# Rotary embedding in one mixer: tables that carry the norm's factors, and two tiles in work

## The chip, the cores and the metric

The kernel runs on one core of a Trainium2 chip. The metric is the device time of one execution in microseconds, as the median of several runs. The engines are TensorE (PE; its weight loads are PEld), VectorE (DVE), ScalarE (ACT), GpSimd (POOL) and the DMA queue of SyncE (SP). Each works through its instructions in program order; they meet at semaphores.

## The reference, cut to what matters

The whole computation is a transformer of several blocks on 16 + 512 tokens: two hybrid layers, then two more mixers, each followed by an MLP and an embedding gate. The change touches one mixer alone, the first of the second half. There the normed input is multiplied by a matrix of 3072 columns; queries and keys of two attentions (4 heads with two maps of 64, and 8 heads of 64) get a rotary embedding over their 64 dimensions:

```python
def rms(x, g):
    y = xf * lax.rsqrt(jnp.mean(xf * xf, axis=-1, keepdims=True) + EPS) * g

def rope_2(x, pos):                      # cos, sin: (position, 32)
    x1, x2 = x[..., :half], x[..., half:]
    return jnp.concatenate([x1 * cos - x2 * sin, x1 * sin + x2 * cos], axis=-1)
```

The first attention takes the difference of two softmax maps per head (a paired attention), the second is a dilated one.

## The kernel before

Activations lie transposed in SBUF: 128 features by up to 528 tokens. A product is computed in fp32 accuracy from two halves: weights and activations are split into a high part and a low part, and each step of a product is three matmuls (high x high, low x high, high x low), lines 1807 to 1809, for outputs of features by tokens, or 1803 to 1805 for outputs of tokens by features (the values). One *step* takes one block of 128 input features; a tile of 128 output features by 512 tokens has eight steps, that is 24 matmuls, in one PSUM bank.

Weights come in panels of 128x512. ScalarE makes the high part of a panel (L1247), VectorE the low part (L1426), TensorE uses it. `begin_panel(j)` puts the split of panel j + 2 into both queues, so a split stands in these queues behind whatever was put there first. A product of one 128-column tile has two panels; a value product (`gemm_tok`, four tiles of tokens by 512 columns, 96 matmuls) has eight.

One function, `schedule`, walks the whole program, and each engine keeps its own part of what `do(...)` names, in that order. `mark()` notes how much each engine has been given up to there; waiting on an engine's mark means waiting until it has done all of that.

The norm's factors (one for each token, the row tile `rs`) are not applied to the input: they are multiplied into each product as it leaves PSUM. For queries and keys this is part of `rope64` (L450). For a tile it issues:

- on ScalarE (L1310): a copy of the tile from PSUM to the second half of `tmp` (L1315), and four copies of 32 partitions each, with neighbouring groups of 32 exchanged, to the first half (L1317). They wait for the product, and for VectorE's mark `prior`, which is all that VectorE was given before. The bank is free when the copies are done.
- on VectorE (L1470): straight part times cos (L1474), crossed part times sin (L1475), their sum (L1477), and the sum times `rs` into the query or key tile (L1479).

All tiles use the same two halves of `tmp`. The mixer (`mixer_ab`, L953) has 16 such tiles. Four query tiles (Q) are computed together by `chunk_major`, under the norm's sums; `lead` (L283) then puts out their four rotary parts and lets four steps of the key products (K) run after each of them. The order of the rotary tiles is Q0 K0 Q1 Q2 K1 Q3 K2 K3. Two value products follow. Then `attend` (L322) runs the paired attention in 16 units of one head and 128 queries, and between their scores, transposes and products it lets steps of `others()` (L1018) run: the eight rotary tiles of the second attention, 64 steps in all. There the VectorE part of a tile is held back in the list `later` until four steps of the next product are out. During this attention the steps use two PSUM banks in turn, elsewhere seven.

In the attention VectorE takes scores with mask and minimum from PSUM (L1626), ScalarE makes exponentials (L1355), VectorE mixes the two maps (L1677 to L1681), TensorE transposes (L1869), VectorE and ScalarE in turn copy the transposes to `PT` (L1640, L1366), and TensorE multiplies with the values (L1881).

The same `rope64` serves the two hybrid layers, which the change leaves as they are.

Of the kernel before, what the change touches and what calls it, by code (L numbers as in the profile page):

```python
# [8 lines left out]
ALU = mybir.AluOpType  # L9
AF = mybir.ActivationFunctionType  # L10
# [4 lines left out]
S = 512  # L15
# [73 lines left out]
def schedule(m, PP, does):  # L89
# [351 lines left out]
    rs = m["rs"]  # L441
# [8 lines left out]
    def rope64(ps, dst, a, b, t, before, later=None):  # L450
# [7 lines left out]
        else:  # L458
            later.append(rest)
        return ("act", "rope64 in", n)  # L460

    def rope32(ps, row, dst, a, b, t, r, before):
# [490 lines left out]
    def mixer_ab(hr, N, produce):  # L953
# [4 lines left out]
        def rotated(dst, o, c, later=None):  # L958
            def evac(ps, a, b, t):
                return rope64(ps, dst[:, o + c, :], a, b, t, before, later=later)  # L960
            return evac
# [256 lines left out]
def scalar_program(act, panels, m, A):  # L1218
# [91 lines left out]
    def rope64_in(it):  # L1310
# [5 lines left out]
        for x in range(4):  # L1316
            e.activation(it.p[32 * x:32 * x + 32], it.ps[32 * (x ^ 1):32 * (x ^ 1) + 32, :], AF.Copy).then_inc(*act.up("rope64 in", it.n))  # L1317

    def zgate(it):
        act.wait_ge("dve", "evac", it.n)  # L1320
        e.activation(it.g, it.zz, AF.Tanh, scale=0.5).then_inc(*act.up("zgate", it.n))
# [73 lines left out]
    def mark(it):  # L1395
        act.note("mark", it.n)

    does = {"mark": mark, "load": load, "load p": load_p, "load lam": load_lam, "split": split, "square": square, "sqrt soon": sqrt_soon, "norm_col": norm_col, "norm_rows": norm_rows,
            "high": high, "copy_out": copy_out, "four_out": four_out, "two_heads": two_heads, "rope64 in": rope64_in, "zgate": zgate, "gate": gate,
            "forget exp": forget_exp, "forget ln": forget_ln, "relu2": relu2, "ple": ple, "scores": scores, "turn": turn, "turn_v": turn_v,  # L1400
# [8 lines left out]
def vector_program(dve, panels, m):  # L1409
# [60 lines left out]
    def rope64(it):  # L1470
# [7 lines left out]
        dve.wait_ge("dve")  # L1478
        e.tensor_tensor(it.dst, it.p, it.rs, ALU.mult).then_inc(*dve.up("rope64", it.n))  # L1479

    def rope32(it):
# [261 lines left out]
    def mark(it):  # L1743
        dve.note("mark", it.n)

    does = {"mark": mark, "load": load, "split": split, "norm_col": norm_col, "norm_rows": norm_rows, "add squares": add_squares, "low": low, "normed": normed, "scale_out": scale_out,
            "two_heads": two_heads, "rope64": rope64, "rope32": rope32, "straight": straight, "crossed": crossed, "zgate": zgate, "gate": gate,
            "proj": proj, "add_quarter": add_quarter, "forget in": forget_in, "forget sum": forget_sum, "forget rows": forget_rows,
# [314 lines left out]
```

## Time and profile before

| | us |
|---|---|
| median of 3 runs | 3099.63 |
| lowest, highest | 3090.12, 3103.06 |
| the profiled execution | 3102.26 |
| its span, first to last instruction | 3100.1 |

| engine | busy us | share of the span | instructions |
|---|---|---|---|
| TensorE, matmuls | 2851.4 | 92% | 15420 |
| TensorE, weight loads | 2380.8 | 77% | 15420 |
| VectorE | 1598.8 | 52% | 3374 |
| ScalarE | 1227.8 | 40% | 2672 |
| GpSimd | 32.2 | 1% | 32 |

A matmul's row reaches beyond the start of the next, since matmuls are pipelined; the distance of two starts tells what one costs. "Idle before" is the time in which an engine stood still before an instruction, with the instruction that released it. The granted clock (PEclk) is the share of full speed that TensorE was given; its mean over the whole execution is 0.949. The chain of waits is followed back from the last instruction, at each step to what released it, so that its shares tell which engine set the end. The mixer's rotary tiles lie between 1516 and 1728 us of the span.

### The profile page before, as it was taken

Reading aid. Unit: us, or ns where it says so; the run is one execution under the profiler, and the core shown is the slowest. Engines: PE = TensorE matmul, PEld = TensorE weight load, DVE = VectorE, ACT = ScalarE, POOL = GpSimd, SP = SyncE. Lnnn points to the kernel's source line nnn. Section 1 sums busy time; section 2 is a strip of 40 time slices with the busy share of each in tenths; the row PEclk is TensorE's granted clock in tenths of the full one; section 3 lists DMA queues with packets and bytes.
Section 4 is the critical chain, followed back from the end, with each engine's and each line's share of the span. In section 5 each row is a group of like instructions: output and inputs, shape, how many; then the busy total and the mean of one; then the engine's idle time right before and its main releaser. Section 6 shows DMA issues by size and latency. Waiting matters only on the chain.

```text
span 3100.1 us, 40010 instructions
## 1 busy us (share of the span) xinstructions
PE 2851.4 (92%) x15420; PEld 2380.8 (77%) x15420; DVE 1598.8 (52%) x3374; ACT 1227.8 (40%) x2672; POOL 32.2 (1%) x32
## 2 busy tenths in 40 slices
PE   7998998999999998999698889999997789899998
PEld 7888988899888777778575567888775477778886
DVE  6354555555444554555447554444556754534445
ACT  3335334433233534433446543333343344433333
POOL 0000000000000000000000000000000000000000
PEclk9999999999998999999898899999997589999999
DMA  3201112122210212223121122333221011233332
GB/s 125 73 21 59 55 42 72 52 76 88 80 52 21 76 44 65 65 75 96 51 77 34 31 65 85 96 95 95 82 70 47 3 40 35 68 94 97 97 96 87
DMA packets 116989, 207.83 MB, mean 67 GB/s; under 512 B 14016, under 2 KB 25152, under 8 KB 116672
## 3 DMA queue, kind: packets, MB, share of 16 engines
q1 hardware_dynamic: 115648, 201.09, 21.6%
q10 hardware_dynamic: 1152, 4.20, 0.4%
q8 instruction: 121, 1.98, 0.3%
q14 instruction: 68, 0.56, 0.1%
HBM read 203.07 MB, written 2.10 MB: 66 GB/s over the span
## 4 chain that ended last, share of the span: by engine, by line
PE 73%; DVE 15%; ACT 9%; issue 2%; DMA 0%; SPq 0%; DVEq 0%; ACTq 0%
PE pp L1807 18%; PE pp L1809 18%; PE pp L1808 17%; PE pp L1881 5%; PE pp L1857 4%; DVE wl L1426 3%; PE pp L1869 2%; ACT tmp L1317 2%; ACT wh L1247 2%; PE pp L1803 1%; PE pp L1804 1%; PE pp L1805 1%; ACT P L1355 1%; PE pp L1914 1%; DVE st L1732 1%
## 5 line engine op out<-in xcount | busy, mean ns | idle before, releaser
L1807 PE MATMUL pp<-Hh,wh 128*128 128x512 f32 (+1 forms) x2322 | 885.1, 381 | 115.7 <-DVE wl L1426 68.8
L1808 PE MATMUL pp<-Hl,wh 128*128 128x512 f32 (+1 forms) x2322 | 813.8, 350 | 0.0
L1809 PE MATMUL pp<-Hh,wl 128*128 128x512 f32 (+1 forms) x2322 | 813.6, 350 | 0.0
L1426 DVE TENSOR_TENSOR wl<-raw,wh 128x512 fp32r<-128x512 f32 (+2 forms) x786 | 507.2, 669 | 459.5 <-ACT wh L1247 446.9
L1807 PEld LDWEIGHTS pp<-Hh,wh 128*128 128x128 f32 x2322 | 454.5, 196 | 220.8 <-DVE wl L1426 81.9
L1247 ACT ACTIVATE wh<-raw 128x512 fp32r<-128x512 f32 (+2 forms) x786 | 454.6, 603 | 264.3 <-PE pp L1809 203.8
L1808 PEld LDWEIGHTS pp<-Hl,wh 128*128 128x128 f32 x2322 | 455.0, 196 | 57.6 <-issue 9.0
L1809 PEld LDWEIGHTS pp<-Hh,wl 128*128 128x128 f32 x2322 | 452.9, 195 | 54.4
L1807 PE MATMUL pp<-Yh,wh 128*128 128x512 f32 (+1 forms) x1280 | 481.5, 376 | 6.7 <-DVE Yl L1446 5.7
L1808 PE MATMUL pp<-Yl,wh 128*128 128x512 f32 (+1 forms) x1280 | 459.0, 359 | 0.0
L1809 PE MATMUL pp<-Yh,wl 128*128 128x512 f32 (+1 forms) x1280 | 458.9, 359 | 0.0
L1355 ACT ACTIVATE P<-P,st 128x256 f32<-128x256 f32 (+7 forms) x280 | 149.9, 535 | 401.9 <-DVE st L1626 401.6
L1807 PEld LDWEIGHTS pp<-Yh,wh 128*128 128x128 f32 x1280 | 242.2, 189 | 51.3 <-DVE Yl L1446 8.0
L1809 PEld LDWEIGHTS pp<-Yh,wl 128*128 128x128 f32 x1280 | 241.8, 189 | 35.7
L1808 PEld LDWEIGHTS pp<-Yl,wh 128*128 128x128 f32 x1280 | 242.4, 189 | 34.1 <-issue 2.2
L1881 PEld LDWEIGHTS pp<-V,PT 128*128 128x128 f32 x1600 | 224.4, 202 | 25.4 <-DVE O L1654 7.2
L1881 PE MATMUL pp<-V,PT 128*128 128x64 f32 (+1 forms) x1600 | 225.3, 277 | 6.1 <-DVE O L1654 3.7
L1857 PE MATMUL pp<-K,Q 64*128 64x256 f32 (+16 forms) x624 | 200.2, 478 | 21.6 <-DVE Z L1523 8.5
L1869 PE MATMUL pp<-con,P 128*128 128x128 f32 x616 | 121.6, 288 | 28.6 <-DVE PT L1640 17.7
L1869 PEld LDWEIGHTS pp<-con,P 128*128 128x128 f32 x616 | 79.1, 146 | 65.6 <-DVE PT L1640 25.0
L1340 ACT ACTIVATE Yh<-tmp 128x512 fp32r<-128x512 f32 x64 | 40.4, 632 | 189.7 <-DVE tmp L1583 189.7
L1857 PEld LDWEIGHTS pp<-K,Q 64*128 64x128 f32 (+2 forms) x624 | 82.6, 203 | 36.6 <-issue 24.9
(219 smaller groups left out, 2672.4 us busy)
## 6 DMA issues: line engine op xcount, KB each, us to landing
raw<-in_w SPq DMA_DIRECT2D x700, 256.0 KB, 2.7
raw<-in_w SPq DMA_DIRECT2D x46, 192.0 KB, 2.4
raw<-in_w SPq DMA_DIRECT2D x40, 128.0 KB, 2.0
out<-X SPq DMA_DIRECT2D x8, 256.0 KB, 2.0
con<-in_con ACTq DMA_DIRECT2D x1, 1576.0 KB, 11.5
X<-in_x SPq DMA_DIRECT2D x2, 528.0 KB, 5.8
X<-in_x ACTq DMA_DIRECT2D x2, 528.0 KB, 6.9
Z<-in_p ACTq DMA_DIRECT2D x2, 512.0 KB, 3.3
```

Of the source, the lines that this page charges most:

```text
L1247: e.activation(part("wh", j), landing(j), AF.Copy).then_inc(*act.up("split", j))
L1317: e.activation(it.p[32 * x:32 * x + 32], it.ps[32 * (x ^ 1):32 * (x ^ 1) + 32, :], AF.Copy).then_inc(*act.up("rope64 in", it.n))
L1340: e.activation(it.hi, it.q, AF.Square).then_inc(*act.up())
L1355: e.activation(p.p, p.p, AF.Exp, bias=p.neg, scale=-1.0, accum_out=p.sum).then_inc(*act.up("exp", it.u))
L1426: e.tensor_tensor(part("wl", j), landing(j), part("wh", j).bitcast(F), ALU.subtract).then_inc(*dve.up("split", j))
L1732: e.max(it.best, it.score).then_inc(*dve.up())
L1807: e.matmul(it.ps, wh, xh, start=it.first, stop=False)
L1808: e.matmul(it.ps, wh, xl, start=False, stop=False)
L1809: e.matmul(it.ps, wl, xh, start=False, stop=it.end).then_inc(*pe.up())
L1857: e.matmul(p.sc, p.q, p.k[:, p.cut:it.ext], start=True, stop=True).then_inc(*pe.up("scores", it.u, x))
L1869: e.transpose(it.b4[:, 128 * x:128 * x + 128], it.p[:, o:o + 128], it.ident).then_inc(*pe.up("turn", it.u))
L1881: done = e.matmul(it.o, p, v, start=x == 0, stop=x == n - 1)
```

## The change

A second form of the rotary step is used in this mixer only. Before the mixer's first tile, VectorE multiplies the cos and the sin table (512 tokens each) by `rs` in place: two operations of 128x512. A tile then needs four copies on ScalarE (the crossed ones, `halves in`), and three operations on VectorE (`rope halves`): crossed part times sin in place, the product's bank times cos into the query or key tile, and the sum of both. The straight copy and the multiplication by `rs` are gone.

The tiles use the two halves of `tmp` in turn. ScalarE's copies of a tile wait for the product and for the sum of the tile two before; those of the first two tiles wait for the tables. VectorE's first operation waits for the copies and for its own last operation. The bank is free when the operation that reads it (`rope straight`) is done.

```diff
+    def rope_scaled(ps, dst, a, b, t, before, later=None):
+
+        x = ropes["n"] % 2
+        p = tmp[:, x, 0:b - a]
+        n = do("halves in", ps=ps, p=p, t=t, prior=ropes["begin"] if ropes["n"] < 2 else None, given=ropes.get(x))["n"]
+        ropes["n"] += 1
+        ropes[x] = n
+
+        def rest():
+            do("rope halves", ps=ps, p=p, cos=cos[:, a:b], sin=sin[:, a:b], dst=dst, n_in=n, before=before)
+        if later is None:
+            rest()
+        else:
+            later.append(rest)
+        return ("dve", "rope straight", n)
...
         def rotated(dst, o, c, later=None):
             def evac(ps, a, b, t):
-                return rope64(ps, dst[:, o + c, :], a, b, t, before, later=later)
+                if "begin" not in ropes:
+                    do("ropes", tables=[cos[:, 0:S], sin[:, 0:S]], rs=rsS)
+                    ropes["begin"] = mark()
+                return rope_scaled(ps, dst[:, o + c, :], a, b, t, before, later=later)
...
+    def halves_in(it):
+        act.wait_ge(*it.t)
+        if it.prior is not None:
+            for other in ("dve", "pe"):
+                act.wait_ge(other, "mark", it.prior)
+        if it.given is not None:
+            act.wait_ge("dve", "rope halves", it.given)
+        for x in range(4):
+            e.activation(it.p[32 * x:32 * x + 32], it.ps[32 * (x ^ 1):32 * (x ^ 1) + 32, :], AF.Copy).then_inc(*act.up("halves in", it.n))
...
+    def ropes(it):
+        for table in it.tables:
+            e.tensor_tensor(table, table, it.rs, ALU.mult).then_inc(*dve.up())
+
+    def rope_halves(it):
+        dve.wait_ge("act", "halves in", it.n_in)
+        for other in ("pe", "act", "pool"):
+            dve.wait_ge(other, "mark", it.before)
+        dve.wait_ge("dve")
+        e.tensor_tensor(it.p, it.p, it.sin, ALU.mult).then_inc(*dve.up())
+        e.tensor_tensor(it.dst, it.ps, it.cos, ALU.mult).then_inc(*dve.up("rope straight", it.n_in))
+        dve.wait_ge("dve")
+        e.tensor_tensor(it.dst, it.dst, it.p, ALU.add).then_inc(*dve.up("rope halves", it.n_in))
```

## Rows read from the trace of the kernel before

**Rows 1.** the page, part 4: the chain that ended last, shares by engine

```profile
PE 73%; DVE 15%; ACT 9%; issue 2%; DMA 0%; SPq 0%; DVEq 0%; ACTq 0%
```

**Rows 2.** busy time by stretch (start:end, length, engines' busy us, PEclk, DMA share)

```profile
1516.40:1561.20 44.80, 22.61 (x73) 16.62 (x72) 21.83 (x34) 24.83 (x42) 0.00 (x0) 0.77 0.08 23
1561.20:1606.70 45.50, 45.48 (x192) 37.00 (x192) 14.36 (x26) 18.75 (x30) 0.00 (x0) 0.96 0.36 105
1606.70:1728.50 121.80, 92.72 (x392) 63.72 (x392) 81.63 (x192) 71.93 (x150) 0.00 (x0) 0.87 0.13 35
```

**Rows 3.** chain of work from 1516.4 to 1561.2, its shares by line

```profile
by line: ACT tmp L1317 36.9%; DVE tmp L1477 11.0%; DVE tmp L1474 10.8%; issue 9.7%; DVE tmp L1475 9.6%; ACT tmp L1315 9.1%; DVE wl L1426 7.8%; DVE Q L1479 3.3%; PE pp L1803 1.5%; ACT rs L1273 1.3%; PE pp L1836 0.3%; DVE K L1479 0.2%; DVEq L
```

**Rows 4.** groups, 1516.4 to 1561.2: line, count, busy, mean, idle before

```profile
L1807 PE MATMUL pp<-Hh,wh 128*128 128x512 f32 x24 | 12.3, 513 | 20.2 <-DVE wl L1426 20.2
...
L1315 ACT ACTIVATE tmp<-pp 128x512 f32<-128x512 f32 x7 | 4.2, 597 | 16.8 <-DVE wl L1426 11.1 <-DVE Q L1479 5.8
```

**Rows 5.** timeline, ScalarE: start, length (us), what, [idle before, releaser]

```profile
1516.44 0.60 ACT L1273 ACTIVATE rs<-pp 128x512 f32<-128x512 f32 x1 [2.14 <-PE pp L1836]
1516.93 0.59 ACT L1315 ACTIVATE tmp<-pp 128x512 f32<-128x512 f32 x1
...
1522.86 0.60 ACT L1315 ACTIVATE tmp<-pp 128x512 f32<-128x512 f32 x1 [2.88 <-DVE Q L1479]
1523.48 2.42 ACT L1317 ACTIVATE tmp<-pp 32x512 f32<-32x512 f32 x4
1525.93 0.63 ACT L1247 ACTIVATE wh<-raw 128x512 fp32r<-128x512 f32 x1
```

**Rows 6.** timeline, VectorE, first query tile and the split after the second tile

```profile
1520.08 0.69 DVE L1474 TENSOR_TENSOR tmp<-tmp,con 128x512 f32<-128x512 f32 x1 [5.57 <-ACT tmp L1317]
1520.69 0.69 DVE L1475 TENSOR_TENSOR tmp<-tmp,con 128x512 f32<-128x512 f32 x1
1521.41 0.69 DVE L1477 TENSOR_TENSOR tmp<-tmp 128x512 f32<-128x512 f32 x1
1522.13 0.69 DVE L1479 TENSOR_TENSOR Q<-tmp,rs 128x512 f32<-128x512 f32 x1
...
1528.60 0.68 DVE L1426 TENSOR_TENSOR wl<-raw,wh 128x512 fp32r<-128x512 f32 x1
```

**Rows 7.** timeline, TensorE, matmuls at either level and the first value product

```profile
1530.36 0.63 PE L1809 MATMUL pp<-Hh,wl 128*128 128x512 f32 x1
1530.79 0.63 PE L1807 MATMUL pp<-Hh,wh 128*128 128x512 f32 x1
...
1536.14 0.40 PE L1808 MATMUL pp<-Hl,wh 128*128 128x512 f32 x1
1536.37 0.40 PE L1809 MATMUL pp<-Hh,wl 128*128 128x512 f32 x1
...
1561.17 0.69 PE L1803 MATMUL pp<-wh,Hh 128*128 128x512 f32 x1 [2.00 <-DVE wl L1426]
```

**Rows 8.** one line's instructions: count, duration ns min/median/max, starts, form

```profile
L1460 DVE TENSOR_TENSOR Q<-pp,rs x5: 681/684/693, 2299.0 to 2303.9; 128x512 f32<-128x512 f32 x5
```

**Rows 9.** groups of the attention stretch, 1606.7 to 1728.5

```profile
L1426 DVE TENSOR_TENSOR wl<-raw,wh 128x512 fp32r<-128x512 f32 x16 | 11.0, 690 | 29.6 <-ACT wh L1247 29.5
...
L1315 ACT ACTIVATE tmp<-pp 128x512 f32<-128x512 f32 x8 | 4.8, 596 | 4.3 <-DVE PT L1640 1.5 <-DVE M L1681 1.4 <-PE pp L1809 1.1
```

**Rows 10.** timeline, ScalarE, before the second tile's copies in the attention

```profile
1627.98 0.19 ACT L1355 ACTIVATION_READ_ACCUMULATOR M<-M,st 128x1 f32 x1
1628.59 0.60 ACT L1315 ACTIVATE tmp<-pp 128x512 f32<-128x512 f32 x1 [0.42 <-DVE M L1681]
```

**Rows 11.** timeline, TensorE, first step of the product after tile 2

```profile
1625.55 0.39 PE L1807 MATMUL pp<-Hh,wh 128*128 128x512 f32 x1
```

**Rows 12.** timeline, VectorE, second operation of tile 1 in the attention

```profile
1621.53 0.69 DVE L1475 TENSOR_TENSOR tmp<-tmp,con 128x512 f32<-128x512 f32 x1
```

**Rows 13.** chain of work, 1606.7 to 1728.5, the piece at the seventh tile

```profile
1716.84 1.12 PE pp L1889 x4
```

More of the change, by code:

```diff
@@ L460, in rope64 @@
         return ("act", "rope64 in", n)
+    ropes = {"n": 0}
+    def rope_scaled(ps, dst, a, b, t, before, later=None):
[11 more added lines that the diff above has]
+        return ("dve", "rope straight", n)
     def rope32(ps, row, dst, a, b, t, r, before):
@@ L1398, in scalar_program @@
     does = {"mark": mark, "load": load, "load p": load_p, "load lam": load_lam, "split": split, "square": square, "sqrt soon": sqrt_soon, "norm_col": norm_col, "norm_rows": norm_rows,
-            "high": high, "copy_out": copy_out, "four_out": four_out, "two_heads": two_heads, "rope64 in": rope64_in, "zgate": zgate, "gate": gate,
+            "high": high, "copy_out": copy_out, "four_out": four_out, "two_heads": two_heads, "rope64 in": rope64_in, "halves in": halves_in, "zgate": zgate, "gate": gate,
             "forget exp": forget_exp, "forget ln": forget_ln, "relu2": relu2, "ple": ple, "scores": scores, "turn": turn, "turn_v": turn_v,
@@ L1746, in vector_program @@
     does = {"mark": mark, "load": load, "split": split, "norm_col": norm_col, "norm_rows": norm_rows, "add squares": add_squares, "low": low, "normed": normed, "scale_out": scale_out,
-            "two_heads": two_heads, "rope64": rope64, "rope32": rope32, "straight": straight, "crossed": crossed, "zgate": zgate, "gate": gate,
+            "two_heads": two_heads, "rope64": rope64, "ropes": ropes, "rope halves": rope_halves, "rope32": rope32, "straight": straight, "crossed": crossed, "zgate": zgate, "gate": gate,
             "proj": proj, "add_quarter": add_quarter, "forget in": forget_in, "forget sum": forget_sum, "forget rows": forget_rows,
```

## The prediction

> **What bounds the kernel now.** The page comes first: TensorE holds 73% of the chain that ended last, VectorE (DVE) and ScalarE (ACT) 24% together [rows 1]. So a gain can only lie where those two carry the chain. The change touches the first mixer of the second block alone, so I looked at that by stretches [rows 2]: from 1516.4 to 1561.2 us TensorE is busy for 22.6 of 44.8 us; from 1561.2 to 1606.7, where the two value products run, it is never idle; from 1606.7 to 1728.5, the paired attention with eight more rotary tiles beside it, it is busy for 92.7 of 121.8 us. The middle stretch has nothing to give.
>
> In the first stretch the chain is nearly all rotary work: the four crossed copies (L1317) 36.9%, the straight copy (L1315) 9.1%, the VectorE lines 1474 to 1479 most of the rest, TensorE under 2% [rows 3]. TensorE waits 20.2 us there for split weights (L1426), and the straight copies wait 16.8 us for VectorE [rows 4]. The reader is to see a ring with one tile in it: ACT copies five times (0.62 + 2.45 us), VectorE works through four operations, and only then does ACT start the next tile; the weight splits stand in the same two queues behind the tiles, so TensorE gets a panel only once per turn. Start to start a tile takes 1522.86 - 1516.93 = 5.9 us, with a split about 6.5 [rows 5, 6].
>
> **First stretch, step by step.** Durations: four crossed copies 2.45 us, one split on ACT 0.65 [rows 5], on VectorE 0.69; a VectorE operation with no wait in front starts 0.61 after the one before, with a wait 0.72 [rows 6]. The new tile is sin (no predecessor in the way), cos 0.61 later, the sum 0.72 later, 0.69 long: 2.02 us against 2.74 from 1520.08 to the end of L1479. New here is that cos reads PSUM. The nearest row is an operation of the same shape that takes PSUM and a table, 684 ns [rows 8], as long as the one from SBUF [rows 6], so I take no difference; the ends are 681 and 693 ns. The Trainium skill, page "VectorE: DVE Perf Modes", section on the TRN2 errata, speaks against this edit: it gives a PSUM source 120 fixed cycles against 58 for SBUF, an estimate of 0.065 us an operation, some 0.9 us over all tiles on the path. The trace does not show that difference.
>
> The tables: two operations of 128x512, placed before the first tile, whose copies wait for them. The norm's row copy ends at 1517.04 [rows 5], so they run to about 1517.1 + 0.61 + 0.69 = 1518.4, and the first copy starts at 1518.45 instead of 1516.93. Nothing hides these 1.5 us; queued behind the waiting ACT is all that follows. The scaled tables serve no later reader with other needs.
>
> From there both queues can be written down, since ACT no longer waits for the tile before (a tile waits for the sum of the tile two before, in its own half of tmp). The order is Q0 K0 split Q1 split Q2 K1 split Q3 split K2 split. ACT: seven tiles of 2.45 and five splits of 0.65 from 1518.45, so K2's copies end at 1538.2. VectorE needs 2.0 a tile and follows about 2 us behind: Q0 is done at 1522.95 and Q1 starts on ACT at 1524.0, Q1 is done at 1528.5 and K1 starts at 1529.55, and so on; no slot holds ACT up, the nearest margin being about 1 us. The splits reach TensorE at 1526.1, 1529.2, 1534.8, 1537.9 and 1541.0; the last is the one that the value product waits for, at 1561.17 before [rows 7]. TensorE itself has two panels of twelve matmuls after 1534.8. A matmul starts every 0.23 us at the granted 2.4 GHz and every 0.43 at 1.2 GHz [rows 7]. All at the higher level it is done in time (1540.7), all at the lower one at 1545.0. TensorE still pauses 2 to 4 us between panels, so I take the mean grant of this stretch before, 0.77 [rows 2]: 24 x 0.23 / 0.77 = 7.2 us, and the value product at 1542.0. The gain is 19, with bounds of 16 and 20.2. Late next is then TensorE.
>
> ACT's last key tile falls beside the value product as before, 5.3 us from copies to the next split against 6.4; two value panels take 5.5, so that stays covered. PSUM banks come free with cos on VectorE instead of with the copies on ACT: with seven banks in turn the first reuse is the last key tile, long after.
>
> **Attention stretch.** Its chain is ACT and VectorE in alternation, one rotary tile for every second head: the copies keep the weight split behind them in ACT's queue, VectorE stands at that split's low half 29.6 us in total [rows 9], and the scores queue behind it. On this chain each of eight tiles loses the straight copy, 8 x 0.62 = 5.0 us. Each loses one of four VectorE operations: the intervals 0.61 + 0.72 + 0.72 + 0.61 become 0.11 (a new wait in front) + 0.61 + 0.72 + 0.61, so 0.61 less; seven of the eight lie on the chain, while at the seventh tile it runs through the transposes instead [rows 13]: 4.3 us. Third, the copies no longer wait for all that VectorE has queued, softmax mixing and PT copies included: 4.3 us of idle time before L1315, of which 1.1 was TensorE's and stays [rows 9]; one such wait is the 0.42 us at 1628.59, where ACT had ended its exponentials and the product had ended before [rows 10, 11]. Of the 3.1 I take 2.5, since at the first tile the product ends just as the copies start. Sum: 5.0 + 4.3 + 2.5 = 11.8.
>
> A new wait comes in: in this stretch the steps have two banks, so the product after next waits for cos, which is held back for four steps, while before it waited for the copies. The product after tile 1 starts at 1625.55 [rows 11], and the second VectorE operation of tile 1 ends at 1621.53 + 0.69 = 1622.2 [rows 12]. This is 3.3 us of cover, and cos itself comes earlier now. I cost it at nothing; if TensorE ran two steps further ahead it would show. Bounds for the stretch: 5 (cover gone, or TensorE late) and 13.2.
>
> **Sum.** 19 + 11.8 = 31 us, 1.0%. The profiled execution took 3102.3 us with a span of 3100.1; it would become about 3071. The median of before is 3099.6, so 3069 is the forecast, and its runs lie between 3090 and 3103.
>
> **Rivals.** *The slots free nothing.* If ACT still had to wait for the tile before in both stretches (through order in the queues, or banks), only the removed operations count: seven tiles x 1.23 - 1.5 = 7.1, and 9.3 in the attention: 16.4, time 3083. For it speaks that each queue is strictly in order; against it, that the walk above finds every wait met. Chance 0.07.
>
> *TensorE takes over in the attention.* It is idle 29.1 us of that stretch and the change asks for 11.8 of them, but the granted clock there is 0.87 [rows 2]. Were it 0.80, its work would be 8 us longer, which leaves 4 of the gain: 19 + 4, time 3077. Against it: VectorE hardly waits for a product in this stretch. Chance 0.13.
>
> *Slower, by the clock.* The grant falls after TensorE idled, and each matmul started at the lower level costs 0.20 us more [rows 7]. The value products have 192 matmuls, nearly all at the higher level [rows 2], and the attention's steps 192 more. If the new, denser pattern of short pauses left the lower level standing through them, 155 matmuls undo the gain, and from 235 the kernel is slower by over 0.5%; all 384 give +77 - 31, time 3146. Against it: the change takes away idle time of TensorE, and before, after waits of 20.2 us in all, the level was low at 1530.36 and high again at 1536.14 [rows 4, 7]. Chance 0.03.
>
> The forecast has the remaining 0.77.
>
> **How the numbers follow.** Best ends together: 20.2 + 13.2 + 1.8 (the value products at a grant of 1.00 instead of 0.96, 45.5 x 0.04 [rows 2]) = 35, time 3064; worst: 16 + 5 = 21, time 3079. With the scatter of the runs shown that gives 3057 to 3084, which takes in the first two rivals. A measurement of this kernel can tell about 0.5%, here 15.5 us, so faster means under 3084: 0.88; within 0.5%: 0.09, mostly the first rival's upper side; slower 0.03.
>
> **What would show it.** In the profile after: (1) copies of the first two query and key tiles back to back, starting about 1.5 us after the norm's rows; (2) the value product at about 25 us after that row copy instead of 44; (3) the product with cos at 0.68 to 0.69 us; (4) in the attention VectorE's idle time before the split's low half down from 29.6 to near 22, and no TensorE wait for the line of cos; (5) a stretch of about 110 us. The forecast is wrong if TensorE waits there for VectorE's cos, if copies still start only after the sum of the tile before, or if the granted clock falls in the value products.

## The result, and the profile after

The changed kernel takes **3073.15 us** (median of five runs, 3066.20 to 3079.09) against 3099.63 for the one before (five runs of the same comparison): ratio 0.9914, 95% interval 0.9895 to 0.9933, which is 26.5 us less. The profiled execution took 3075.13 us with a span of 3073.3. Two later comparisons of the same kernel gave 0.9884 and 0.9875; what lies between these figures has a section below.

The page of after, part 4 (shares of the chain that ended last):

```profile
PE 75%; DVE 14%; ACT 8%; issue 2%; DMA 0%; SPq 0%; DVEq 0%; ACTq 0%
```

VectorE and ScalarE together go from 24% [rows 1] to 22% of a span that is 27 us shorter, so what went away came out of their part of the chain. The same three stretches as [rows 2], in after (start:end, length, then busy us and count for PE, PEld, DVE, ACT, POOL, then granted clock, DMA share, GB/s):

```profile
1516.10:1540.56 24.46, 18.90 (x73) 14.08 (x72) 18.27 (x29) 20.80 (x36) 0.00 (x0) 0.93 0.15 43
1540.56:1584.40 43.84, 43.82 (x192) 35.96 (x192) 13.78 (x25) 18.12 (x29) 0.00 (x0) 1.00 0.37 108
1584.40:1693.60 109.20, 84.34 (x392) 58.75 (x392) 76.74 (x184) 67.11 (x142) 0.00 (x0) 0.97 0.14 39
```

The same work took 44.8, 45.5 and 121.8 us before. In the first of them ScalarE goes from 42 to 36 instructions and VectorE from 34 to 29, and ScalarE is now busy for 20.8 of 24.5 us. The granted clock rose in all three: 0.77 to 0.93, 0.96 to 1.00, 0.87 to 0.97.

From here on I read every kernel by three distances that don't depend on where the window is cut: **first** is from the end of the norm's row copy [rows 5] to the first value product [rows 7], **values** from there to the first score matmul of the paired attention, **attention** from there to the first score of the second attention. Before they are 44.13, 46.34 and 121.03, sum 211.5. After they are 23.83, 44.64 and 108.43, sum 176.9.

ScalarE's timeline of after over the first stretch (start, length in us, engine and line, what, [idle before, releaser]; L1348 are the crossed copies, L1268 the high half of a split):

```profile
1516.13 0.60 ACT L1294 ACTIVATE rs<-pp 128x512 f32<-128x512 f32 x1 [2.14 <-PE pp L1881]
1518.10 4.88 ACT L1348 ACTIVATE tmp<-pp 32x512 f32<-32x512 f32 x8 [1.36 <-DVE con L1514]
1523.00 0.63 ACT L1268 ACTIVATE wh<-raw 128x512 fp32r<-128x512 f32 x1
1523.65 2.42 ACT L1348 ACTIVATE tmp<-pp 32x512 f32<-32x512 f32 x4
1526.10 0.63 ACT L1268 ACTIVATE wh<-raw 128x512 fp32r<-128x512 f32 x1
1526.76 4.88 ACT L1348 ACTIVATE tmp<-pp 32x512 f32<-32x512 f32 x8
```

After the 1.36 us for the two scaled tables there is no idle bracket left: Q0's and K0's copies stand together as one row of eight. Compare [rows 5], where 2.88 us lie between two tiles. VectorE in the same stretch (L1521 sin, L1522 cos from PSUM, L1524 sum, L1457 low half of a split):

```profile
1520.56 0.69 DVE L1521 TENSOR_TENSOR tmp<-tmp,con 128x512 f32<-128x512 f32 x1 [2.50 <-ACT tmp L1348]
1521.16 0.68 DVE L1522 TENSOR_TENSOR Q<-pp,con 128x512 f32<-128x512 f32 x1
1521.88 0.69 DVE L1524 TENSOR_TENSOR Q<-Q,tmp 128x512 f32<-128x512 f32 x1
1523.00 0.69 DVE L1521 TENSOR_TENSOR tmp<-tmp,con 128x512 f32<-128x512 f32 x1 [0.43 <-ACT tmp L1348]
...
1524.94 0.68 DVE L1457 TENSOR_TENSOR wl<-raw,wh 128x512 fp32r<-128x512 f32 x1
...
1539.82 1.29 DVE L1457 TENSOR_TENSOR wl<-raw,wh 128x512 fp32r<-128x512 f32 x2
```

From the second tile on VectorE waits 0.4 to 0.5 us for each tile's copies, so ScalarE alone now sets the pace: 2.42 a tile and 0.63 a split, with hardly a gap. On TensorE, the pause ahead of the fourth of the five panels and the step to the value product (same columns):

```profile
1534.34 0.50 PE L1852 MATMUL pp<-Hh,wh 128*128 128x512 f32 x1 [1.29 <-DVE wl L1457]
1534.68 0.39 PE L1853 MATMUL pp<-Hl,wh 128*128 128x512 f32 x1
1534.91 0.40 PE L1854 MATMUL pp<-Hh,wl 128*128 128x512 f32 x1
...
1540.09 0.39 PE L1854 MATMUL pp<-Hh,wl 128*128 128x512 f32 x1
```

The starts are 0.23 us apart after the first, the upper level of [rows 7], and the granted clock from 1534.34 to 1540.56 us is 1.00. The end of the chain of waits over this stretch (start, length, who) tells what released the value product:

```profile
1539.56 0.25 PE pp L1854
1539.82 0.69 DVE wl L1457
1540.52 0.04 issue
1540.56 0.50 PE pp L1848
```

TensorE was through with its last key panel at about 1540.3, and the split for the value product ended at 1540.5: the split is the last to arrive, by 0.2 us. TensorE's waits for split weights, 1516.1 to 1540.6 (us in total, times, longest), against the 20.2 of [rows 4]:

```profile
PE pp L1852 <- DVE wl L1457: 5.4, 2, 4.1
```

Groups of the attention stretch of after, 1584.4 to 1693.6 (count | busy us, mean ns | idle before, releasers), beside [rows 9]:

```profile
L1348 ACT ACTIVATE tmp<-pp 32x512 f32<-32x512 f32 x32 | 18.8, 588 | 2.0 <-PE pp L1854 1.3
L1457 DVE TENSOR_TENSOR wl<-raw,wh 128x512 fp32r<-128x512 f32 x16 | 11.0, 690 | 22.8 <-ACT wh L1268 22.7
L1522 DVE TENSOR_TENSOR Q<-pp,con 128x512 f32<-128x512 f32 x4 | 2.7, 685 | 0.0
```

The idle time ahead of ScalarE's copies fell from 5.1 us (4.3 ahead of the straight ones, 0.8 ahead of the crossed ones) to 2.0; of what is left 1.3 us is a wait for TensorE, the rest gaps of 0.02 us, and no wait for VectorE is named; the wait at the split's low half fell from 29.6 to 22.8.

### The profile page after: what moved, and what is told of

It reads as the page before. It is cut to its first block, busy times and chain, and to the rows that moved or that the text cites. A ratio compares the mean times of both kernels' runs of the same rounds, so it can differ in the third digit from the quotient of the medians.

```text
span 3073.3 us, 39979 instructions
## 1 busy us (share of the span) xinstructions
PE 2850.2 (93%) x15420; PEld 2381.4 (77%) x15420; DVE 1589.5 (52%) x3360; ACT 1218.5 (40%) x2656; POOL 32.0 (1%) x32
## 3 DMA queue, kind: packets, MB, share of 16 engines
q8 instruction: 121, 1.98, 0.3%
## 4 chain that ended last, share of the span: by engine, by line
PE 75%; DVE 14%; ACT 8%; issue 2%; DMA 0%; SPq 0%; DVEq 0%; ACTq 0%
PE pp L1852 19%; PE pp L1854 18%; PE pp L1853 18%; PE pp L1926 5%; PE pp L1902 4%; DVE wl L1457 2%; PE pp L1914 2%; ACT wh L1268 1%; PE pp L1848 1%; PE pp L1850 1%; PE pp L1849 1%; PE pp L1959 1%; ACT tmp L1348 1%; ACT P L1386 1%; DVE st L1777 1%
## 5 line engine op out<-in xcount | busy, mean ns | idle before, releaser
L1457 DVE TENSOR_TENSOR wl<-raw,wh 128x512 fp32r<-128x512 f32 (+2 forms) x786 | 507.1, 668 | 456.8 <-ACT wh L1268 442.5
L1268 ACT ACTIVATE wh<-raw 128x512 fp32r<-128x512 f32 (+2 forms) x786 | 454.7, 603 | 264.1 <-PE pp L1854 206.2
L1637 DVE TENSOR_TENSOR M<-pp,M 128x512 f32<-128x512 f32 x56 | 38.7, 692 | 139.0 <-PE pp L1854 138.0
```

Source lines behind the costliest of these rows:

```text
L1268: e.activation(part("wh", j), landing(j), AF.Copy).then_inc(*act.up("split", j))
L1457: e.tensor_tensor(part("wl", j), landing(j), part("wh", j).bitcast(F), ALU.subtract).then_inc(*dve.up("split", j))
L1637: e.tensor_tensor(it.y, it.ps, it.y, ALU.add).then_inc(*dve.up("evac", it.n))
```

## The experiments

The theory: the first stretch gains about 19 us, from a ring with one tile in it that becomes two full queues; the attention gains about 12, from one copy and one VectorE operation less for each tile, and from a wait for VectorE's whole queue that became a wait for one instruction. The rivals that the runs had to exclude: only the removed operations count; the overlap alone counts; the later stretches take or give something of their own.

| kernel | median us (n) | ratio to before, 95% | first | values | attention | of it the last wait | sum |
|---|---|---|---|---|---|---|---|
| before | 3099.63 (5) | | 44.13 | 46.34 | 121.03 | 1.15 | 211.5 |
| after | 3073.15 (5) | 0.9914, 0.9895 to 0.9933 | 23.83 | 44.64 | 108.43 | 0.90 | 176.9 |
| after_again | 3062.63 (4) | 0.9884, 0.9850 to 0.9917 | 23.84 | 44.68 | 107.55 | 0.02 | 176.1 |
| after_paired | 3067.46 (6) | 0.9875, 0.9848 to 0.9903 | 23.85 | 44.66 | 108.62 | 1.09 | 177.1 |
| lead_only | 3079.04 (6) | 0.9936, 0.9907 to 0.9964 | 23.85 | 44.64 | 121.06 | 0.90 | 189.6 |
| attention_only | 3086.04 (10) | 0.9969, 0.9946 to 0.9991 | 44.15 | 46.33 | 110.03 | 1.07 | 200.5 |
| one_tile | 3081.03 (10) | 0.9934, 0.9913 to 0.9956 | 33.70 | 44.64 | 108.61 | 1.07 | 187.0 |
| queue_wait | 3077.80 (8) | 0.9926, 0.9901 to 0.9952 | 23.85 | 44.65 | 111.73 | 1.36 | 180.2 |
| straight_copy | 3078.74 (8) | 0.9930, 0.9900 to 0.9959 | 28.21 | 44.68 | 113.65 | 1.98 | 186.5 |
| plain_tables | 3067.23 (3) | 0.9915, 0.9855 to 0.9975 | 25.46 | 44.70 | 113.71 | 0.35 | 183.9 |
| early_tables | 3065.14 (3) | 0.9913, 0.9866 to 0.9960 | 22.51 | 44.64 | 109.34 | 1.80 | 176.5 |
| all_rotary | 3049.34 (5) | 0.9815, 0.9790 to 0.9839 | 22.52 | 44.64 | 109.21 | 1.66 | 176.4 |

The first two rows are one comparison. Three later ones had their own runs of before, with medians of 3103.40 (21 runs), 3098.20 (17) and 3105.27 us (10). The first of them holds after_again, one_tile, attention_only and lead_only, the second queue_wait, straight_copy, plain_tables and early_tables, the third after_paired and all_rotary. The whole times scatter by 6 to 25 us within a kernel. Much of that comes before the mixer: its row copy ends anywhere from 1503.2 to 1519.6 us in the eleven profiles in which everything ahead of it is the same. The distances repeat within 0.02 us in the first stretch, 0.07 in the values and about 1.1 in the attention.

The attention's scatter has one place. The *last wait* in the table is the idle time of ScalarE ahead of its copies for the eighth and last rotary tile, whose product TensorE is still computing. These copies and that idle time, in after_again, after and early_tables:

```profile
1686.12 2.42 ACT L1348 ACTIVATE tmp<-pp 32x512 f32<-32x512 f32 x4
1689.01 2.42 ACT L1348 ACTIVATE tmp<-pp 32x512 f32<-32x512 f32 x4 [0.90 <-PE pp L1854]
1676.91 2.42 ACT L1348 ACTIVATE tmp<-pp 32x512 f32<-32x512 f32 x4 [1.80 <-PE pp L1854]
```

The granted clock from the copies of the seventh tile to these is 1.00, 0.85 and 0.72:

```profile
1675.55:1686.12 10.57, 6.73 (x35) 5.10 (x33) 6.26 (x11) 6.31 (x11) 0.00 (x0) 1.00 0.08 31
1677.56:1689.01 11.45, 6.80 (x29) 5.16 (x27) 7.05 (x12) 6.31 (x11) 0.00 (x0) 0.85 0.11 30
1664.57:1676.91 12.34, 7.68 (x29) 5.83 (x27) 7.04 (x12) 6.31 (x11) 0.00 (x0) 0.72 0.07 26
```

Without this wait the attention takes 107.53 us in each of the three executions of after, and 107.54 to 107.55 in one_tile, early_tables and all_rotary; before takes 119.88. So the attention too can be compared to some hundredths of a microsecond, and I call this its *net* distance. The distances carry the verdicts below, and the ratios say only that the wholes agree with them.

**after_again and after_paired** are the changed kernel unedited, run beside the kernels of the first and of the third later comparison.

> The changed kernel once more, nothing edited, to tell what belongs to it from what belongs to one execution. The local gain of 34.6 us (first product stretch 20.3, value products 1.7, attention 12.6) should come back within 0.5 us in the first and third part, which no TensorE level decides. My theory of the missing 8 us (two later stretches of 435 and 438 us, the same instructions in both kernels, took 3.9 us more each at a lower granted clock) says that these differ from execution to execution: in this profile they should lie anywhere between 435 and 442 us, and the kernel at 3066 to 3079 us. The rival says that the change causes them, by moving what follows against the clock's rhythm: then they are 438.8 and 441.5 us again.

> The changed kernel beside the next one, with more rounds, for the size of its gain over many executions. Expected from the parts: 34.6 to 35.4 us off the mixer in every execution, while later stretches scatter by some us with the granted clock: median about 35 us under that of the kernel before, ratio 0.989. If the 26.5 us of the first comparison were the whole gain, the ratio would be 0.9915 again.

Measured: 176.1 and 177.1 against 176.9. The gain in the mixer is 34.4 to 35.4 us in all three executions, whatever the whole shows. Two expectations missed: after_again's attention is 0.9 us shorter than after's, where I had allowed 0.5 (it is the last wait, 0.02 against 0.90), and its whole times, 3060 to 3066 us, lie below the 3066 to 3079 that I had named. The interval of after_paired, 0.9848 to 0.9903, excludes the 0.9915 of its rival.

**lead_only and attention_only** each do one half of the change: the new form for the tiles of the first attention alone (o == 0), or of the second alone (o == 4). In lead_only the attention's tiles still go through `rope64`, on tables that carry the norm's factor already, so the factor enters twice in them; the operations and their order are those of before. In attention_only the tables are scaled at the first tile inside the attention, and the scaling has a wait for VectorE's own last operation in front (not in the excerpt).

```diff
         def rotated(dst, o, c, later=None):
             def evac(ps, a, b, t):
+                if o == 4:      # lead_only; attention_only has o == 0
+                    return rope64(ps, dst[:, o + c, :], a, b, t, before, later=later)
                 if "begin" not in ropes:
```

> The new form in the first stretch only; the attention's eight tiles take the old five copies and four operations (their output carries the norm's factor twice, since the tables are scaled). Theory: first stretch 23.8 us, attention 121.0 us, time about 3099.6 - 20.3 - 1 = 3078. Rival: attention shorter than 118 us although its work is the old one, which would put part of its gain down to the earlier start.

> The eight tiles of the first stretch keep the old five copies and four operations, the tables are scaled when the attention's first tile comes. Theory (the two gains are independent and add up): first stretch 44.1 us, attention 108.4 us plus up to 1.4 for the tables' two operations, time about 3099.6 - 11 = 3088. Rival (the attention gained only because it began in another state): attention near 121 us, time 3100.

Measured: lead_only 23.85 and 121.06, attention_only 44.15 and 110.03. Each has one half at the value of after and the other at that of before (lead_only's net attention, 120.16, within 0.3 us). attention_only pays for the tables there: its net attention is 108.96, 1.4 us over that of after; its values last 46.33 as before, so the 1.7 us that the value products gain belong to the first stretch. The granted clock goes with it; attention_only, first stretch and values:

```profile
1504.90:1549.45 44.55, 22.71 (x71) 16.60 (x71) 21.80 (x34) 24.64 (x42) 0.00 (x0) 0.73 0.09 24
1549.45:1595.78 46.33, 45.51 (x192) 37.05 (x193) 14.39 (x26) 19.45 (x31) 0.00 (x0) 0.96 0.35 103
```

With the old first stretch the value products start after TensorE idled half of the time, and their mean grant is 0.96; in after it is 1.00, from the first matmul.

**one_tile** keeps the new operations but gives every tile the same half of `tmp`, so a tile's copies wait for the sum of the tile before.

```diff
-        x = ropes["n"] % 2
+        x = 0
...
-        n = do("halves in", ps=ps, p=p, t=t, prior=ropes["begin"] if ropes["n"] < 2 else None, given=ropes.get(x))["n"]
+        n = do("halves in", ps=ps, p=p, t=t, prior=ropes["begin"] if ropes["n"] < 1 else None, given=ropes.get(x))["n"]
```

> All tiles use the same half of tmp, so ScalarE's copies of a tile wait for the sum of the tile before; tables and operation counts stay. Theory (overlap is most of the gain in the first stretch, and nothing of it in the attention, where one tile comes every 13 to 16 us): from the norm's rows to the value product 37 us (44.1 less 7 x 1.23, plus 1.5 for the tables) instead of 23.8, attention 108.4 as before, time 3086. Rival (removed operations are the gain, in either stretch): first stretch stays at about 24 to 26 us, time 3073 to 3076.

Measured: 33.70 in the first stretch, 108.61 in the attention. So the second half of `tmp` is worth 9.9 us where tiles stand in a row and nothing in the attention (net 107.54 against 107.53). The first figure is 3.3 us under what I expected. ScalarE and VectorE of one_tile show why, from the second tile on:

```profile
1511.35 2.43 ACT L1348 ACTIVATE tmp<-pp 32x512 f32<-32x512 f32 x4 [2.09 <-DVE Q L1524]
1513.80 0.63 ACT L1268 ACTIVATE wh<-raw 128x512 fp32r<-128x512 f32 x1
1515.86 2.42 ACT L1348 ACTIVATE tmp<-pp 32x512 f32<-32x512 f32 x4 [1.43 <-DVE K L1524]
```

```profile
1515.13 0.69 DVE L1524 TENSOR_TENSOR K<-K,tmp 128x512 f32<-128x512 f32 x1
1515.74 0.68 DVE L1457 TENSOR_TENSOR wl<-raw,wh 128x512 fp32r<-128x512 f32 x1
```

A turn takes 1515.86 - 1511.35 = 4.5 us, copies to copies. The copies start when the sum ends (1515.13 + 0.69), while the split's low half (1515.74) is still running. Before, the copies waited for VectorE's mark, and the split stood under it: of the 16.8 us that they waited, 11.1 were for L1426 [rows 4]. I had taken only the removed operations out of the ring and left the low half in it. The seven turns, from copies to copies and the last to the value product, took 5.93, 6.46, 6.46, 5.93, 6.46, 6.52 and 6.48 us before and take 4.52, 4.51, 4.51, 4.58, 4.51, 4.57 and 5.14 here. The two turns without a split lose 1.35 to 1.41 us, which is the copy's 0.62 and the 0.72 of the fourth operation; my 1.23 had counted 0.61 for that one. The last turn loses 1.34, although it holds a split, because the value product itself waits for its low half. The other four lose 1.95 each, so the narrower wait takes out 0.6 in each of them. Of the 3.3 us some 1.0 is thus the removed work, which I had priced too low, and 2.3 the narrower wait. No run puts the old wait back in this stretch, so this split between the two rests on the turns alone. Both together are worth 44.13 - 33.70 = 10.4 us, net of 1.5 for the tables, and the second slot 9.9.

**queue_wait** puts the old wait back for the attention's eight tiles: ScalarE also waits for all that VectorE was given before.

```diff
-        n = do("halves in", ps=ps, p=p, t=t, prior=ropes["begin"] if ropes["n"] < 2 else None, given=ropes.get(x))["n"]
+        n = do("halves in", ps=ps, p=p, t=t, all_of=mark() if ropes["n"] >= 8 else None, prior=ropes["begin"] if ropes["n"] < 2 else None, given=ropes.get(x))["n"]
...
+        if it.all_of is not None:
+            act.wait_ge("dve", "mark", it.all_of)
```

> Only for the eight tiles in the attention, ScalarE's copies wait again for everything that VectorE was given before. Theory (this wait was a part of its own in the attention's gain, priced at 2.5 us of the 3.1 shown): first stretch 23.8 us, attention 110.5 to 111.3 us against 107.6 and 108.4 in the two profiles of the changed kernel, time about 3 us more. Rival (the wait was hidden by the order of ScalarE's queue): attention stays at 107.6 to 108.4.

Measured: 111.73, which is 3.1 to 4.2 above the three executions of after (and 2.4 above early_tables, run beside it). The group of the crossed copies in queue_wait, same stretch:

```profile
L1350 ACT ACTIVATE tmp<-pp 32x512 f32<-32x512 f32 x32 | 18.8, 589 | 5.4 <-DVE PT L1687 1.8 <-DVE M L1728 1.4 <-PE pp L1856 1.4
```

The copies idle 3.4 us more than in after (5.4 against 2.0); 3.2 of the 5.4 are waits for the PT copies and the mixing of the maps. Not all of that is a loss: the last wait is 1.36 here and 0.90 in after, and at the first tile the copies waited 0.42 for TensorE in after anyway and wait 0.78 now. The net distance is 110.37, so the wait is worth 2.8 us where I had kept 2.5 of 3.1.

**straight_copy** puts the straight copy back on ScalarE, straight into the query or key tile; cos then reads that copy, and the bank is free after the copies, as before.

```diff
+        for other in ("pe", "dve", "pool"):
+            act.wait_ge(other, "mark", it.before)
+        e.activation(it.dst, it.ps, AF.Copy).then_inc(*act.up())
...
-        e.tensor_tensor(it.dst, it.ps, it.cos, ALU.mult).then_inc(*dve.up("rope straight", it.n_in))
+        e.tensor_tensor(it.dst, it.dst, it.cos, ALU.mult).then_inc(*dve.up("rope straight", it.n_in))
...
-        return ("dve", "rope straight", n)
+        return ("act", "halves in", n)
```

> ScalarE copies the product into the query or key tile first (five copies again), VectorE multiplies it by cos from SBUF, and the bank is free with the copies. Theory (the copy is paid in full, the bank's later release and the PSUM read cost nothing): first stretch 23.8 + 7 x 0.62 = 28.2 us, attention 108 + 8 x 0.62 = 113 us, VectorE's cos operation at 0.68 to 0.69 us in either form. Rival (holding the bank until cos costs TensorE something in the attention): attention 110 us or less, since the earlier release gives that back.

Measured: first stretch +4.4, attention +5.0 to 6.1. Seven tiles times 0.62 are 4.3: in the first stretch each removed copy counts in full. In the attention the difference holds the last wait, 1.98 us here; the net distances, 111.67 against 107.53, give 4.1 for eight copies. From one tile to the next the lag against after grows by 0.47 to 0.50 us up to the seventh. The straight copy is as long as ever, but it starts 0.10 us after the start of the row before it (at the second tile), where the crossed copies of after start 0.21 after theirs. The run decides a second question too. The rival's 110 us or less did not come, and no wait of TensorE for L1522 shows in after, so holding the bank until cos costs nothing that these traces show. And cos from SBUF is no shorter than cos from PSUM; the durations of the query tiles' cos in after, from PSUM, and in straight_copy, from SBUF (ns, min/median/max):

```profile
L1522 DVE TENSOR_TENSOR Q<-pp,con x8: 683/684/687, 1521.2 to 1640.9; 128x512 f32<-128x512 f32 x8
L1525 DVE TENSOR_TENSOR Q<-Q,con x8: 683/684/687, 1524.7 to 1650.3; 128x512 f32<-128x512 f32 x8
```

**plain_tables** leaves the tables alone and multiplies each tile by `rs` as a fourth operation, with two tiles in work as in after. The first two tiles' copies also wait for the transposes that used `tmp` before (not in the excerpt).

```diff
-                    do("ropes", tables=[cos[:, 0:S], sin[:, 0:S]], rs=rsS)
...
         e.tensor_tensor(it.dst, it.dst, it.p, ALU.add).then_inc(*dve.up("rope halves", it.n_in))
+        if it.rs is not None:
+            dve.wait_ge("dve")
+            e.tensor_tensor(it.dst, it.dst, it.rs, ALU.mult).then_inc(*dve.up())
```

> Tables stay as they are, each tile is multiplied by the norm's row at the end (four operations on VectorE, four copies, two tiles in work). Theory: no tables' 1.4 us at the start, but VectorE (2.74 us a tile and 0.69 a split) is now slower than ScalarE (2.45 and 0.65), so the first stretch is about 2.45 + 7 x 2.74 + 5 x 0.69 + 0.2 = 25.2 us; attention 108 + 7 x 0.72 = 113 us. Rival (VectorE's fourth operation is hidden under the copies of the next tile): first stretch 22.5, attention 108.

Measured: first stretch 25.46 (+1.6), attention 113.71 (+5.1 to 6.2). In the attention the net distance is 113.36, 5.8 us more: the fourth operation costs its full 0.72 at each of eight tiles. The seventh is no exception, although I had left it out. In the first stretch the copies start at once, which saves 1.4, so seven such operations cost 3.0 there, 0.43 each. VectorE's timeline in plain_tables shows where that comes from:

```profile
1512.01 0.69 DVE L1522 TENSOR_TENSOR tmp<-tmp,con 128x512 f32<-128x512 f32 x1
...
1514.06 0.69 DVE L1528 TENSOR_TENSOR Q<-Q,rs 128x512 f32<-128x512 f32 x1
1514.67 0.68 DVE L1458 TENSOR_TENSOR wl<-raw,wh 128x512 fp32r<-128x512 f32 x1
1515.46 0.69 DVE L1522 TENSOR_TENSOR tmp<-tmp,con 128x512 f32<-128x512 f32 x1
```

No idle bracket is left from the second tile on: the operation fills the 0.4 to 0.5 us of slack that VectorE had in after and then sets the pace, 1515.46 - 1512.01 = 3.45 us for a tile with its split, against ScalarE's 2.42 + 0.63 and their gaps, 3.1.

**early_tables** lets the first two tiles' copies start without waiting for the tables, which only VectorE needs.

```diff
                 if "begin" not in ropes:
-                    do("ropes", tables=[cos[:, 0:S], sin[:, 0:S]], rs=rsS)
                     ropes["begin"] = mark()
+                    do("ropes", tables=[cos[:, 0:S], sin[:, 0:S]], rs=rsS)
```

> The copies of the first two tiles wait only for what VectorE was given before the two table operations, so these run beside the first copies. Theory (the tables stood on the path with 1.4 us): first stretch 23.8 - 1.4 = 22.4 us, attention unchanged at 107.6 to 108.4. Rival (TensorE or the splits are next in line): first stretch stays above 23.3 us.

Measured: first stretch 22.51, 1.3 us less, the idle time ahead of the first copies. The sum of the three is 176.5, inside the 176.1 to 177.1 of after, because the attention came out at 109.34; all_rotary, with the same edit, has 109.21. All of the excess is the last wait, 1.80 and 1.66 us; the net attention is 107.54 and 107.55, so the edit costs nothing in the seven tiles before. The last wait goes with the granted clock, as shown above. With two profiles of this edit it stays open whether the edit makes the low level likelier there.

**all_rotary** is early_tables with the new form in the two hybrid layers too: four copies, cos from PSUM and two tiles in work there, with `rs` as a fourth operation since their tables serve others as well. The extra wait of plain_tables is in it too; of the layers' tiles the excerpt shows the queries, and the keys get the same call.

```diff
         before = mark()
+        here = {"n": 0, "begin": before}
...
-                    lambda ps, a, b, t, c=c: rope64(ps, Q[:, c, a:b], a, b, t, before)))
+                    lambda ps, a, b, t, c=c: rope_scaled(ps, Q[:, c, a:b], a, b, t, before, ropes=here, rs=rs)))
```

> Two edits beyond the changed kernel: the table operations run beside the first copies (early_tables), and the rotary tiles of the two hybrid layers take four crossed copies with two tiles in work too, keeping plain tables and the multiplication by the norm's row, since these tables serve twice. Theory: 1.3 us from the first; in the layers TensorE waits 10.9 and 7.4 us for weights' low halves beside these tiles, of which I expect 8 to 12 to go, since the copies stop waiting for VectorE's queue; time 10 to 13 us under the changed kernel. Rival (there TensorE feeds the tiles one by one, eight steps each, and only the copy's 0.4 to 0.6 us is saved): 3 us or less.

Measured: 3049.34, ratio 0.9815 (0.9790 to 0.9839), 56 us under before and 18 under after_paired of the same comparison, the fastest of all kernels here. TensorE's waits from 455 to 515 us, in the first hybrid layer (us in total, times, longest), in after_paired and then in all_rotary:

```profile
PE pp L1852 <- DVE wl L1457: 9.2, 5, 2.8
PE pp L1934 <- DVE O L1699: 1.0, 1, 1.0
```

```profile
PE pp L1940 <- DVE O L1705: 1.0, 1, 1.0
```

The five waits for split weights are gone; in the second hybrid layer (1180 to 1250 us) they fall from 7.4 to 0.7. That is 15.9 us, less 2.4 for a new wait of the scores there for a small VectorE operation (L1715), plus the 1.3 of the tables: 14.8 us. The medians differ by 18.1, against the 10 to 13 expected. The 3.3 us between the two are within the scatter of the wholes. I had expected 8 to 12 us of the layers' waits to go; 13.5 net went, since hardly any of them was left.

## Where the first comparison lost eight microseconds

The three stretches gain 34.6 us, the profiled execution as a whole 3102.26 - 3075.13 = 27.1. The rest went in two places that the change doesn't touch, the MLP stretches after the mixer. Before:

```profile
1804.10:2239.00 434.90, 414.20 (x1828) 338.07 (x1827) 203.92 (x319) 157.89 (x285) 0.00 (x0) 0.99 0.30 90
2631.60:3069.20 437.60, 417.21 (x1829) 339.48 (x1828) 203.91 (x319) 157.94 (x286) 0.00 (x0) 0.99 0.29 89
```

The same work in after:

```profile
1769.20:2208.00 438.80, 419.31 (x1829) 342.23 (x1828) 203.85 (x319) 157.93 (x286) 0.00 (x0) 0.98 0.29 89
2600.90:3042.40 441.50, 422.70 (x1829) 344.86 (x1828) 203.89 (x319) 157.92 (x285) 0.00 (x0) 0.97 0.28 89
```

And in after_again, the same program once more:

```profile
1766.30:2201.40 435.10, 414.53 (x1829) 338.21 (x1828) 203.94 (x319) 157.95 (x286) 0.00 (x0) 0.99 0.29 90
2594.10:3031.60 437.50, 417.21 (x1829) 339.47 (x1828) 203.82 (x319) 157.92 (x286) 0.00 (x0) 0.99 0.29 89
```

The counts agree within one record, VectorE's and ScalarE's times within 0.1 us; TensorE's busy time follows the granted clock. After pays 3.9 + 3.9 = 7.8 us there, and 34.6 - 7.8 = 26.8 is the 27.1 within 0.3. After_again pays nothing. The changed kernel in two executions gives both values, and one_tile, plain_tables and the others mix them freely (439.0 then 437.5 in one_tile, 439.1 then 435.9 in plain_tables, 441.5 then 437.3 in early_tables). So the changed kernel need not pay these 8 us. How often before would pay them isn't shown: it was profiled once, and of the eleven profiles of changed kernels ten have 438.8 us or more in the first of the two stretches. What makes the grant dip in one execution and not in the next, no run here tells.

## Why the prediction was right

It said 3069 with 3057 to 3084; measured were 3073.15, 3062.63 and 3067.46, which is 26.5, 40.8 and 37.8 us under the runs of before beside each. The whole times alone don't tell the forecast from its rivals: the range was wide enough to take in the first two (3083 and 3077). The distances do. They also show that the gain of 34.4 to 35.4 us in the mixer lies at my best end (35), not at the 31 of the sum. Point by point:

- **First stretch, 19 foretold, 20.3 measured.** The walk through the queues held: counted from the end of the row copy, the low halves were to end at 9.1, 12.2, 17.8, 20.9 and 24.0 us, and ended at 8.9, 12.0, 17.6, 20.7 and 23.8. The one step that was off is TensorE's clock, and with it the order of arrival: not TensorE came last but the split, as in the bound. I took the mean grant of before, 0.77, for the last two panels; they ran at the upper level throughout, so the value product came at 23.8 us, not at 25. The reason given for 0.77, pauses of 2 to 4 us, was wrong too: the pauses before those panels are 1.3 us and less.
- **The tables, 1.4 to 1.5 us that nothing hides**: 1.36 measured, and early_tables shows that 1.3 of it needn't be there.
- **cos from PSUM at no extra cost**: 684 ns, as [rows 8] had it. The Trainium skill, page "VectorE: DVE Perf Modes", section on the TRN2 errata, with 120 fixed cycles for PSUM against 58 would, by an estimate from these two figures, have made it about 0.065 us longer. The trace doesn't agree: 683 to 687 ns from PSUM and from SBUF alike.
- **Attention, 11.8 foretold, 12.6 measured** (12.4 to 13.5 over three executions). Without the last wait of either kernel it is 119.88 - 107.53 = 12.35 us, and the last wait itself (1.15 us before, 0.02 to 1.09 after) makes the rest. The three terms were not as right as their sum: the copies, put at 5.0, are worth 4.1 (straight_copy); the wait for the whole queue, put at 2.5, 2.8 (queue_wait). If the parts add up, the operation is left with 12.35 - 4.1 - 2.8 = 5.4, where I had 4.3; put back, with its wait, it costs 5.8 (plain_tables), and at all eight tiles, not seven. Copy and operation were off by 0.9 and 1.1 us in opposite directions, and that they cancel is luck. The 13.5 of after_again lies just over the bound of 13.2, whose terms the prediction doesn't give.
- **No cost for the longer hold of the bank**: straight_copy gains nothing from the early release, and no wait of TensorE for L1522 appears in after.
- **The value products**: their 1.7 us stood only in the best case; they came in every kernel with the new first stretch and not in attention_only. The step that failed is again the clock, which I let rise in a bound and not in the sum.
- **The sum**: 20.3 + 12.6 + 1.7 = 34.6 against 31. The profiled execution of the first comparison gained 27.1 and not 34.6 because of the 7.8 us of clock in the MLPs, which no step had; that the median too came out above 3069, not below, is likely the same, but only one of its runs was profiled.
- **The rivals.** That the slots free nothing (16.4 in all) is excluded for the first stretch by one_tile, where the second slot is worth 9.9. Its price was too low: a turn without a split loses 1.35 to 1.41 us in one_tile, not 1.23. In the attention it is right as far as it goes: the slot is worth nothing there, and what counts is the two operations and the wait. TensorE did not take over: the granted clock there was 0.97, 0.92 and 0.96 in the three executions of after, and the net distance was the same. Only at the first and the last tile do the copies wait for it, 0.4 us and up to 1.1 us in these three; in straight_copy the last wait is 1.98. The price of that rival didn't follow from its terms either, since 8 us more of work and the 11.8 us asked for fit into the 29.1 us of idle time. The slower case needed the lower level to stand through the value products; their grant is 1.00.

My separation of causes was less sure than the sum. I spoke of a ring that becomes two queues, and half of the 20 us comes without any second slot: the shorter tile, and the wait that no longer holds the split's low half, which the prediction has for the attention and not here.

## What to carry to other kernels

Where one engine waits for another's whole queue, list what stands under that mark, weight splits included: narrowing the wait to the one instruction that matters gained 2.3 us in the first stretch (read from the turns, with one tile in work) and 2.8 in the attention (queue_wait), where the removed copies gained 4.4 and 4.1. A second buffer pays only where tiles stand in a row (9.9 us) and nothing where other work lies between them (0.0), and then the fuller engine alone sets the pace. Where whole times scatter by more than the effect, measure from one instruction to another: a distance that repeats within 0.02 us tells one part of a change from another when ratios with an interval of 0.4% can't. Where a distance scatters, look for the one wait that takes up the scatter, before the scatter is used as an error bar: here it hid that the copies were worth 4.1 and not 5.0.

## What the runs showed of the hardware

TensorE's grant over long stretches without any difference in the program varies between executions: the same 1828 or 1829 recorded matmuls took 434.9, 435.1 or 438.8 us at 0.99, 0.99 and 0.98, and as many later 437.5 or 441.5 us at 0.99 and 0.97. Over all profiles here these two stretches lie between 434.3 and 444.0 us; the first is 435.0 to 435.1, 438.8 to 439.1 or 441.5 and nothing between. These steps of 3 to 4 us are as large as many effects that one wants to measure. And a pause of 1.29 us before a panel left TensorE at the upper level: the matmul after it took 0.34 us to the next start, and from there on 0.23. A pause of 4.10 us in the same trace was followed by starts 0.34 to 0.23 us apart at first, from 1525.68 on; from 1527.09 they were 0.43 apart, the lower level, and from 1530.36 on 0.23 again, so the grant fell only after TensorE had started again.
